# A decoder layer with expert retrieval: all late U slots in two fp32r parts, eight row fetches before the one-hots, nine per group

## The reference

```python
def _peer(h, w_q, sub_keys, exp_u, exp_v):          # h: 256 tokens x 2048
    q = einsum('td,de->te', xb, w_q).reshape(tb, 8, 2, 128)
    s = einsum('thcd,hckd->thck', q, sub_keys)       # 128 keys per half
    sv, si = top_k(s, 16)
    cand = sv[:, :, 0, :, None] + sv[:, :, 1, None, :]          # 16 x 16 pairs
    cidx = si[:, :, 0, :, None] * 128 + si[:, :, 1, None, :]
    top_v, top_j = top_k(cand, 16)                   # 8 heads x 16 experts a token
    eidx = take_along_axis(cidx, top_j)
    gw = softmax(top_v)
    a = gelu(einsum('td,thkd->thk', xb, exp_u[eidx]))
    return einsum('thk,thkd->td', gw * a, exp_v[eidx])
# then h = layernorm(2**0.25 * h + peer(h))
```

## Time and profile before

| | before |
|---|---|
| median of 3 runs | 1977.45 us (1972.92 to 1978.24) |
| profiled execution | 1972.88 us, its span 1971.1 us |
| PE busy | 1915.7 us (97%) |
| DVE busy | 1339.1 us (68%) |
| ACT busy | 735.1 us (37%) |
| POOL busy | 303.1 us (15%) |
| HBM traffic | 530.74 MB read, 277 GB/s over the span |

### The profile page before, as it was taken

One profiled execution on the slowest core, in us unless ns is written; L12 is line 12 of the kernel. 1 busy time (PEld: TensorE's weight loads), 2 busy tenths in 40 slices (PEclk: granted clock), 3 DMA queues, 4 the chain that ended last, 5 costly groups with the idle time before them and its releaser, 6 DMA issues.

```text
span 1971.1 us, 27293 instructions
## 1 busy us (share of the span) xinstructions
PE 1915.7 (97%) x11300; PEld 1728.3 (88%) x11300; DVE 1339.1 (68%) x1896; ACT 735.1 (37%) x917; POOL 303.1 (15%) x216
## 2 busy tenths in 40 slices
PE   7999999999879999999999999999999999999996
PEld 7998999789779999998777889889899899898894
DVE  5334454567564496995888776876877877877746
ACT  4324555444343101223445333433433433433432
POOL 1000123000000000101222222212322322322000
PEclk9989999999989999999999999999999999999998
DMA  7545433755343765898998899999999999999951
GB/s 302 193 177 186 150 129 107 286 183 220 123 145 113 268 261 207 293 353 292 328 337 324 336 360 349 400 362 357 392 359 366 395 351 369 394 350 371 379 208 52
DMA packets 124540, 548.33 MB, mean 278 GB/s; under 512 B 58000, under 2 KB 58064, under 8 KB 60160
## 3 DMA queue, kind: packets, MB, share of 16 engines
q1 hardware_dynamic: 52928, 374.36, 49.7%
q0 software_dynamic: 20096, 147.04, 19.8%
q10 hardware_dynamic: 51392, 25.17, 4.5%
HBM read 530.74 MB, written 14.68 MB: 277 GB/s over the span
## 4 chain that ended last, share of the span: by engine, by line
PE 96%; DVE 2%; ACT 1%; DMA 0%; issue 0%; SPq 0%; POOL 0%; DVEq 0%; ACTq 0%
PE bank L554 17%; PE bank L889 12%; PE bank L794 11%; PE bank L569 10%; PE bank L880 7%; PE bank L825 6%; PE bank L824 6%; PE bank L828 6%; PE bank L826 6%; PE bank L827 6%; PE bank L882 3%; PE bank L814 2%; PE bank L592 1%; DVE hres L1398 1%; PE bank L648 1%; DMA ring_raw<-in_stream 0%
## 5 line engine op out<-in xcount | busy, mean ns | idle before, releaser
L1228 DVE TENSOR_TENSOR ring_lo<-ring_raw,ring_hi 128x2048 fp32r<-128x2048 f32 (+1 forms) x96 | 211.3, 2202 | 219.8 <-ACT ring_hi L927 219.6
L554 PE MATMUL bank<-actT_hi,ring_hi 128*128 128x256 f32 x912 | 263.7, 289 | 11.3 <-DVE ring_lo L1233 8.6
L554 PE MATMUL bank<-actT_lo,ring_hi 128*128 128x256 f32 x912 | 261.1, 286 | 0.0
L554 PE MATMUL bank<-actT_hi,ring_lo 128*128 128x256 f32 x912 | 261.0, 286 | 0.0
L1597 DVE TENSOR_TENSOR split_a<-experts,split_a 128x2048 fp32r<-128x2048 f32 x97 | 221.7, 2291 | 54.0 <-ACT split_a L1150 53.3
L1150 ACT CAST split_a<-experts 128x2048 fp32r<-128x2048 f32 x97 | 185.6, 1913 | 153.7 <-PE bank L828 151.5
L927 ACT CAST ring_hi<-ring_raw 128x2048 fp32r<-128x2048 f32 (+1 forms) x96 | 176.2, 1836 | 110.0 <-PE bank L569 86.1
L794 PE MATMUL bank<-h2T,experts 128*128 128x192 f32 x1280 | 216.3, 326 | 0.0
L794 PEld LDWEIGHTS bank<-h2T,experts 128*128 128x128 f32 x1280 | 206.9, 190 | 0.0
L554 PEld LDWEIGHTS bank<-actT_hi,ring_hi 128*128 128x128 f32 x912 | 178.3, 195 | 12.0 <-DVE actT_lo L1233 8.0
L526 POOL DMA_INDIRECT rows<-in_peer_v,eidx x64 | 133.2, 2081 | 348.1 <-DVE hrow L1568 315.2
(11 more groups left out here) (251 smaller groups left out, 3695.3 us busy)
## 6 DMA issues: line engine op xcount, KB each, us to landing
experts<-in_stream SPq DMA_DIRECT2D x221, 1024.0 KB, 5.2
ring_raw<-in_stream SPq DMA_DIRECT2D x96, 1024.0 KB, 4.8
late_raw<-in_stream SPq DMA_DIRECT2D x35, 1024.0 KB
gate_matrix<-stage ACTq DMA_DIRECT2D x12, 1024.0 KB
gbuf<-gate_matrix ACTq DMA_DIRECT2D x32, 384.0 KB, 11.0
gb<-in_ln_g POOLq DMA_DIRECT2D x3, 1024.0 KB, 5.5
gb<-in_ln_b POOLq DMA_DIRECT2D x3, 1024.0 KB, 9.6
act_raw<-in_xT SPq DMA_DIRECT2D x4, 512.0 KB, 7.0
```

The costliest lines, as they stand in the source:

```text
L554: last = pe.matmul(bank[n % 2][:, 0:T], ring[w][:, s % R, k * P:(k + 1) * P], act[x][:, k, :], start=(k == 0 and i == 0), stop=(k == KO - ...
L1228: dve.tensor_tensor(ring_lo[:, r, 0:n], ring_raw[:, r, 0:n], ring_hi[:, r, 0:n].bitcast(F32), ALU.subtract).then_inc(lo_ready, 1)
```

## The change

`U_SPLIT` goes from 4 to 8, so all eight U slots of a late group are split. `cross` and `ga` become one tile. DVE uses eight fetches before the one-hots and 12 among them (20 in place of 12), 18 in place of 16 in the early V pass, and nine in place of ten in each late group, three of them in its U half in place of six. The gate matrix is read by eight chunks at a time. The weight's remainders are made in one DVE instruction of 192 columns; ACT gets a second copy of 64 columns instead. The first two weights and one `split_low` change their places at either end of the early V pass. The gelu of the 64 tokens' products moves to group 7, and into its V half.

```diff
-U_SPLIT = 4
+U_SPLIT = 8
-GELU_G = 8
-GELU_I = 6
+GELU_G = 7
+GELU_I = 3
-IN_G, IN_LOADING, IN_V0, IN_LATE = 12, 2, 16, 10
-IN_LATE_U = 6
+IN_CHOICE = 8
+IN_G, IN_LOADING, IN_V0, IN_LATE = 20, 2, 18, 9
+IN_LATE_U = 3
...
-                act.dma_start(gbuf[:, q % 2], gdram[:, :, 4 * q:4 * q + 4, :]).then_inc(g_landed[q % 2], 16)
+                act.dma_start(gbuf[:, q % 2], gdram[:, :, 8 * q:8 * q + 8, :]).then_inc(g_landed[q % 2], 16)
...
+                act.copy(w_split[:, c % 8, 2 * ND:2 * ND + NS], wt[:, c % 2, P:ND])
                 act.copy(w_split[:, c % 8, 0:ND], wt[:, c % 2, :]).then_inc(w_hi, 1)
...
+                if k == N_EARLY - 2:
+                    w_high(0)
+                    w_high(1)
                 if k >= N_EARLY - 2:
                     split_high(k - (N_EARLY - 2) + 1)
-            w_high(0)
-            w_high(1)
...
-                        act.copy(cross[:, i % 2, :], bank[(N_U + i) % 2][:, ND:2 * ND]).then_inc(cross_out, 1)
+                        act.wait_ge(wt_ready, c - 1)
+                        act.copy(ga[:, i % 2, :], bank[(N_U + i) % 2][:, ND:2 * ND]).then_inc(cross_out, 1)
...
+            gathers(IN_CHOICE)
             dve.wait_ge(idx_out, 2)
             for n in range(QUADS):
...
-                gathers(IN_G * (n + 1) // QUADS)
+                gathers(IN_CHOICE + (IN_G - IN_CHOICE) * (n + 1) // QUADS)
...
-                dve.tensor_tensor(w[:, ND:2 * P], whole[:, P:ND], w[:, P:ND].bitcast(F32), ALU.subtract)
-                dve.tensor_tensor(w[:, 2 * P:3 * P], whole[:, 0:P], w[:, 0:P].bitcast(F32), ALU.subtract).then_inc(w_ready, 1)
+                dve.tensor_tensor(w[:, ND:2 * ND], whole, w[:, 0:ND].bitcast(F32), ALU.subtract).then_inc(w_ready, 1)
...
-            split_low(1)
             for c in range(2):
                 dve.wait_ge(tb_out, N_U + c + 1)
                 gated(early_chunk(c), c)
             for c in range(2):
                 w_low(c)
+            split_low(1)
...
-                split_low(c)
+                if m < N_EARLY - 1:
+                    split_low(c)
...
+                if n == 1:
+                    split_low(N_EARLY + 1)
             split_low(N_EARLY + 2)
```

More of the change, by code:

```diff
@@ L250, in build @@
         with ExitStack() as c3:
-            w_split = sb("w_split", [P, 8, 2 * ND], F32R, c3)
+            w_split = sb("w_split", [P, 8, 2 * ND + NS], F32R, c3)
             wt = sb("wt", [P, 2, ND], c=c3)
-            cross = sb("cross", [P, 2, ND], c=c3)
-            gbuf = sb("gbuf", [P, 2, N_STAGE, 4, STAGE_T], F32, c3)
+            gbuf = sb("gbuf", [P, 2, N_STAGE, 8, STAGE_T], F32, c3)
             ga = sb("ga", [P, 2, ND], c=c3)
@@ L824, in split_products @@
                 pe.matmul(whole[:, :], w_split[:, c, 0:P], hi, start=first, stop=False, skip_group_check=True)
-                pe.matmul(whole[:, :], w_split[:, c, 2 * P:3 * P], hi, start=False, stop=False, skip_group_check=True)
-                pe.matmul(rest[:, :], w_split[:, c, P:2 * P], hi, start=fresh, stop=False, skip_group_check=True)
+                pe.matmul(whole[:, :], w_split[:, c, ND:ND + P], hi, start=False, stop=False, skip_group_check=True)
+                pe.matmul(rest[:, :], w_split[:, c, ND + P:ND + 2 * P], hi, start=fresh, stop=False, skip_group_check=True)
                 pe.matmul(whole[:, :], w_split[:, c, 0:P], lo, start=False, stop=final, skip_group_check=True)
@@ L1138, in load_gates @@
                 if q >= 2:
-                    act.wait_ge(wt_ready, 4 * (q - 1))
-                act.dma_start(gbuf[:, q % 2], gdram[:, :, 4 * q:4 * q + 4, :]).then_inc(g_landed[q % 2], 16)
+                    act.wait_ge(wt_ready, 8 * (q - 1))
+                act.dma_start(gbuf[:, q % 2], gdram[:, :, 8 * q:8 * q + 8, :]).then_inc(g_landed[q % 2], 16)
             def split_high(m):
@@ L1156, in w_high @@
                     act.wait_ge(split_used, c - 7 if c < N_EARLY else split_u(c // 8, 0))
+                act.copy(w_split[:, c % 8, 2 * ND:2 * ND + NS], wt[:, c % 2, P:ND])
                 act.copy(w_split[:, c % 8, 0:ND], wt[:, c % 2, :]).then_inc(w_hi, 1)
-                if c % 4 == 3 and c // 4 + 2 < 4 * 8:
-                    load_gates(c // 4 + 2)
+                if c % 8 == 7 and c // 8 + 2 < GROUPS_P:
+                    load_gates(c // 8 + 2)
             early_activation(N_EARLY - WHILE_LOADING)
@@ L1201, in _ @@
                         act.wait_ge(sum_out, U_SPLIT * (g - EARLY_G) + i + 1)
-                        act.wait_ge(wt_ready, c - 1)
-                        act.activation(ga[:, i % 2, :], cross[:, i % 2, :], ACT.Gelu_apprx_tanh).then_inc(ga_ready, 1)
-                    if g == GELU_G and i == GELU_I:
-                        act.wait_ge(row_used, GATHERS)
-                        act.activation(wpair[:], apair[:], ACT.Gelu_apprx_tanh).then_inc(wpair_gelu, 1)
+                        act.activation(ga[:, i % 2, :], ga[:, i % 2, :], ACT.Gelu_apprx_tanh).then_inc(ga_ready, 1)
                 w_high(8 * g + 7)
@@ L1213, in _ @@
                         split_high(split_v(g, i + RH))
+                    if g == GELU_G and i == GELU_I:
+                        act.wait_ge(row_used, GATHERS)
+                        act.activation(wpair[:], apair[:], ACT.Gelu_apprx_tanh).then_inc(wpair_gelu, 1)
                     if g == GROUPS_P - 1 and i % 2:
@@ L1599, in gated @@
             def gated(src, c):
-                if c % 4 == 0:
-                    dve.wait_ge(g_landed[c // 4 % 2], 16 * (c // 8 + 1))
+                if c % 8 == 0:
+                    dve.wait_ge(g_landed[c // 8 % 2], 16 * (c // 16 + 1))
                 if c >= 2:
@@ L1605, in gated @@
                 staged = lambda ap: ap.rearrange("p (s t) -> p s t", s=N_STAGE)
-                dve.tensor_tensor(staged(wt[:, c % 2, :]), staged(src), gbuf[:, c // 4 % 2, :, c % 4, :],
+                dve.tensor_tensor(staged(wt[:, c % 2, :]), staged(src), gbuf[:, c // 8 % 2, :, c % 8, :],
                                   ALU.mult).then_inc(wt_ready, 1)
@@ L1662, in _ @@
                         dve.wait_ge(cross_out, U_SPLIT * (g - EARLY_G) + i + 1)
-                        dve.tensor_tensor(cross[:, i % 2, :], cross[:, i % 2, :], bank[(N_U + i) % 2][:, 0:ND],
+                        dve.tensor_tensor(ga[:, i % 2, :], ga[:, i % 2, :], bank[(N_U + i) % 2][:, 0:ND],
                                           ALU.add).then_inc(sum_out, 1)
```

## The result

The changed kernel takes 2003.57 us (median of 4 runs, 2002.13 to 2008.34) against 1976.45 us of the kernel before (4 runs, 1972.92 to 1978.24). The ratio is 1.0138, 95% interval 1.0118 to 1.0159: slower by 27 us. The profiled execution took 2003.53 us, its span is 2001.6.

The account below looks back on a forecast made before the run. PE bound the profiled kernel; in the changed late groups the order of DVE and ACT would. 1972.9 + 24 + 18 + 2.5 - 10.7 = 2006.7, forecast 2008 us, own range 2000 to 2018, 8-in-10 range 1983 to 2034.

Parts of the forecast that it names:

- Late groups, +24: Late stage: DVE and ACT order makes PE pause, +24 us taken from a range of +18 to +45.
- the walk: One late group stepped through by durations: PE pauses 5.0 us, group 78.1 us; +22 us over all groups.
- a ring of 5.27 us: Late U half: sum, gated, w_high, split_high, split_low to next sum take 5.27 us against PE's 4.55 a slot.
- The allowance of 2 for rows and clock: Late groups: +24 taken over the walk's +22, as late fetched rows or a fallen clock could add time.
- counter-case: Rival for the late groups: PE stays the bound, giving 1943 to 1954 us; chance 0.08.
- Eight uses ahead, +18 and 2.5 of clock: Before the one-hots: PE stands still 18 us for rows still landing, then loses 2.5 us to the lower clock.
- Ends of the early V pass, -10.7: Both ends of that pass: waits of 3.0 and 2.6 us go, with 1.7 and 3.4 us of clock.
- At nothing: Merged w_low, 18 uses in the early V pass, gates by eight: no cost; gelu in group 7: up to 2 us.
- a rule: Skill page: tensor_tensor doesn't hold up descriptor writing, so split_low would not delay POOL's issues; late stage then +22 us.

Follow-up runs that it names:

- Removing the cause: Changed kernel with four split U slots a late group instead of eight: 1984.5 us, ratio 1.0043 to the kernel before.
- the kernel without the known terms: Changed kernel with four split U slots, three uses ahead of the one-hots and the early V pass's ends as before: 1975.5 us, ratio 1.0003.

## Why the prediction was right

The time came out 4.4 us under the forecast of 2008, in its own range, by the mechanism forecast. The terms, one by one:

- **Late groups, +24 (22 of it from the walk).** Predicted a ring of 5.27 us and groups of 78.1; measured 5.20, and 77.8 to 78.0 for all but the first and the last by the starts of sum(0). Predicted pauses at U5 to U7, V0 and V2, which sum to 5.0 a group; measured 77.9 - 73.1 = 4.8 by the lengths of the groups (the list of waits has only 37 / 11 = 3.4 of them). By the starts of the matmuls U5 loses nothing, U6 0.6, U7 0.65, V0 1.7 and V2 1.65 us, where 0.2, 0.7, 0.7, 1.8 and 1.6 were forecast. The walk holds step by step: counted from PE's start of U0, the sums of a group in the middle start at 7.1, 9.6, 14.8, 22.3, 27.5, 32.7, 36.1 and 39.6 us, each within 0.5 of the forecast, and `split_low`(v2) is done at 50.0 instead of 50.4. The stage is longer by 17.0 us, and 3.4 of clock were saved at its start, so +20.4. Removing the cause gave 19 us. The allowance of 2 for rows and clock did not come: the clock stayed at 1.00 in all late groups, and DVE had no waits for rows in the late groups.
- **That the order makes the ring.** The prediction gave as its counter-case that PE stays the bound "if ACT came to split_high without waiting for gated". Two orders turned on ACT did just that: 73.4 to 73.6 us a group, and 73.1 to 73.3 with one use moved on DVE as well, with the same DVE work. This is shown, and it decides between the forecast and that rival.
- **Eight uses ahead, +18 and 2.5 of clock.** Measured 18.3 of pause. Of clock 2.7: the second and third one-hot matmuls come 4.40 and 2.69 us after the one before where the pace is 2.19 (the window says 3.0). The middle of it was less exact than the end: fetch 3 was used at 789.05 instead of 794, since its issue was done at 784.4 and not at 788; fetches 5 and 7 were used at 800.65 and 805.40 (800 and 806 forecast). POOL's timeline of the changed kernel, the gates' transfers, that issue and the two behind it:

```profile
781.61 1.13 POOL L522 DMA_DIRECT2D gpair<-pick  x2 [54.39 <-DVE rows L1563]
783.04 1.36 POOL L526 DMA_INDIRECT rows<-in_peer_u,eidx  x1 [0.30 <-issue]
784.70 1.86 POOL L526 DMA_INDIRECT rows<-in_peer_u,eidx  x1 [0.30 <-issue]
786.87 0.94 POOL L526 DMA_INDIRECT rows<-in_peer_u,eidx  x1 [0.30 <-issue]
```

  The uses held it up by 0.4 us where I had put in about 4 us for it. The landings were wrong the other way: from the end of its issue to its use, fetch 3 took 4.7 us, fetch 4 took 9.1 (786.56 to 795.67) and fetch 5 12.8 (787.81 to 800.65), where the forecast had 6 for each. Issues put too late and landings put too short cancel, so that 18 against 18.3 is in part luck; that the three buffers and the landings make the pause is not.
- **Ends of the early V pass, -10.7.** From the marks: one-hots to first V product 132.0 before, 131.4 after with 2.7 of clock loss in it, so -3.3 for the wait of 3.0; the V pass -4.2, for the wait of 2.6 at its end and the 1.7 of clock at its start; and 3.4 of clock behind it: -10.9. Alone on the kernel before: 10 to 11 us. The only part of the change that gains, and it was hidden under the two losses. Its 5.1 us of clock are those of one execution: with the same pauses, the kernel without the known terms has no fall of the clock at the first V product, and the kernel with eight uses ahead has none at the first late U slot (1.00 from 1130 to 1144 us). So up to 5.1 of the 10.7 depend on the execution that is taken as before.
- **At nothing.** 1.0003 (0.9982 to 1.0024) for the rest.

18.3 + 2.7 - 10.9 + 20.4 = 30.5, the difference of the two spans. The sum of the forecast was 33.8; the 3.3 that it was high are the late groups' 3.6.

POOL's issues, the place where the prediction weighed a rule. POOL's timeline of the changed kernel has an issue that starts under a `split_low`:

```profile
957.54 3.02 POOL L526 DMA_INDIRECT rows<-in_peer_u,eidx  x1 [19.89 <-DVE rows L1563]
```

DVE's timeline has that `split_low`:

```profile
957.46 2.28 DVE L1599 TENSOR_TENSOR split_a<-experts,split_a 128x2048 fp32r<-128x2048 f32 x1
```

The issue takes 3.02 us and ends 0.8 after that instruction. 56 issues of this trace start under a `split_low`, with a median of 2.93 us; those that start under the additions from PSUM (`hres<-hres,bank`) or under nothing take 0.94. The Trainium skill, page "SBUF — State Buffer", section "Who interferes with whom", has it that a `tensor_tensor` doesn't hold up descriptor writing, which it marks as inferred. The trace does not agree: the issue waits, as under the use in the earlier trace rows. Whether it waits to write its descriptors or to read its indices `eidx`, the trace does not tell. The prediction had left this open, and the rows to decide it were in the trace of before, where 60 issues start under a `split_low` with the same median. It cost the late groups nothing: DVE's waits from 1100 us on have none for a fetched row.

## What to carry to other kernels

When a piece of work is added to engines that both have room, walk the order and not the sums: write down which instruction of each engine waits for which of the other, add the turn up once around, and compare it with the pace of the engine that should bound. If the turn is longer, look for a copy that is ready but queued behind one that waits; changing the order of two such instructions was worth 23 us here, of a second pair 19 to 20 more, with no work taken out. And filling an idle stretch of an engine is only free up to what is already there: three fetched rows were, eight were not, and whatever stood behind the fourth paid for its landing.
